# Queries, keys and gate rows stored per head for 128-row loads, y stored before values, and a new order at the start of the merge

## What is computed

```python
h = rmsnorm(x, rms_g) * (1 + scale) + shift
q, k, v, z_a, glu, z_b, gates = jnp.split(h @ w_in + b_in, PROJ_SPLITS, axis=-1)
y_a = attend(q, k, v) * jax.nn.silu(z_a)        # 8 heads of 64
y_b = conv_branch(glu, dw_w, dw_b, ln_g, ln_b) * jax.nn.silu(z_b)
g_a, g_b = jnp.split(jax.nn.sigmoid(gates), 2, axis=-1)
m = g_a * (y_a @ w_proj_a) + g_b * (y_b @ w_proj_b)
return x + gate * (m @ w_out), k, v
```

## Time and profile before

| | us |
|---|---|
| median of 3 runs | 1874.22 (1873.65 to 1875.42) |
| the profiled execution's own time | 1877.82 |
| its span, first to last instruction | 1875.6 |
| TensorE busy | 1829.8 |
| mean granted TensorE clock | 0.997 of full |

### The profile page before, as it was taken

The page is one execution under the profiler, slowest core; times in us unless marked ns, Lnnn a source line. Parts: engine busy times, 40 slices in busy tenths (PEclk is TensorE's granted clock), DMA queues, the critical chain, the costliest instruction groups (busy, mean ns, idle before and its releaser), DMA issues.

```text
span 1875.6 us, 27263 instructions
## 1 busy us (share of the span) xinstructions
PE 1829.8 (98%) x10723; PEld 1561.1 (83%) x10723; DVE 1015.1 (54%) x1710; ACT 542.0 (29%) x1061; POOL 122.8 (7%) x205
## 2 busy tenths in 40 slices
PE   6999999999999999999999999999999899999998
PEld 3788899988888888888888888888888888888886
DVE  3544512111098338816870996766768555654444
ACT  3731101021111111211110114667768222322221
POOL 0100000000000000000000004322330000000000
PEclk9999999999999999999999999999999999999999
DMA  9524423143022112211220164997887767653321
GB/s 318 169 89 158 144 68 132 49 140 115 12 78 89 65 34 82 76 40 59 72 80 20 65 153 119 211 178 163 175 182 176 229 205 244 193 191 140 141 101 56
DMA packets 211145, 235.08 MB, mean 125 GB/s; under 512 B 47707, under 2 KB 157131, under 8 KB 207819
## 3 DMA queue, kind: packets, MB, share of 16 engines
q1 hardware_dynamic: 210760, 233.24, 42.5%
q10 hardware_dynamic: 259, 0.11, 0.0%
HBM read 152.52 MB, written 80.78 MB: 124 GB/s over the span
## 4 chain that ended last, share of the span: by engine, by line
PE 90%; SPq 4%; DMA 2%; issue 1%; ACT 1%; DVE 1%; POOLq 0%; DVEq 0%; POOL 0%; ACTq 0%
PE banks L789 17%; PE banks L790 17%; PE banks L791 17%; PE banks L1742 4%; PE banks L1741 4%; PE banks L1743 4%; PE banks L1713 3%; PE banks L1715 3%; PE banks L1714 3%; PE banks L1225 3%; SPq L1093 2%; PE banks L784 2%; PE banks L785 2%; PE banks L786 2%; PE banks L1191 2%
## 5 line engine op out<-in xcount | busy, mean ns | idle before, releaser
L789 PE MATMUL banks<-h_hi,w_hi 128*128 128x512 f32 (+1 forms) x1600 | 593.3, 371 | 3.6 <-DVE h_lo L598 2.5
L790 PE MATMUL banks<-h_lo,w_hi 128*128 128x512 f32 (+1 forms) x1600 | 589.4, 368 | 0.0
L791 PE MATMUL banks<-h_hi,w_lo 128*128 128x512 f32 (+1 forms) x1600 | 589.3, 368 | 0.0
L730 DVE SCALAR_TENSOR_TENSOR conv_acc<-glu_out,taps,conv_acc 128x773 f32<-128x773 f32 x360 | 371.5, 1032 | 12.3
L789 PEld LDWEIGHTS banks<-h_hi,w_hi 128*128 128x128 f32 x1600 | 301.8, 189 | 57.6 <-issue 3.4
L791 PEld LDWEIGHTS banks<-h_hi,w_lo 128*128 128x128 f32 x1600 | 301.8, 189 | 50.7
L790 PEld LDWEIGHTS banks<-h_lo,w_hi 128*128 128x128 f32 x1600 | 302.0, 189 | 49.0
L506 ACT ACTIVATE out_stage<-banks,param_cols 128x512 f32<-128x512 f32 (+1 forms) x120 | 77.0, 647 | 439.2 <-PE banks L791 433.2
L1713 PE MATMUL banks<-y_hi,wp_hi 128*128 128x512 f32 (+1 forms) x320 | 120.0, 375 | 4.9 <-DVE m_sum L1935 2.8
L1332 ACT ACTIVATE probs<-scores,stat 128x640 f32<-128x640 f32 (+2 forms) x128 | 106.7, 834 | 60.2 <-DVE stat L1259 58.6
L1715 PE MATMUL banks<-y_hi,wp_lo 128*128 128x512 f32 (+1 forms) x320 | 118.4, 370 | 0.0
(11 more groups left out here) (161 smaller groups left out, 2397.5 us busy)
## 6 DMA issues: line engine op xcount, KB each, us to landing
proj<-out_stage SPq DMA_DIRECT2D x96, 256.0 KB, 2.0
w_raw<-in_w_in SPq DMA_DIRECT2D x44, 512.0 KB, 3.9
gates_in<-proj SPq DMA_DIRECT2D x64, 256.0 KB, 2.9
k_hi<-k_hi_rows SPq DMA_DIRECT2D x16, 640.0 KB, 13.2
k_lo<-k_lo_rows SPq DMA_DIRECT2D x16, 640.0 KB, 15.2
w_ada<-in_w_ada SPq DMA_DIRECT2D x8, 1024.0 KB, 10.8
x_out<-in_x_sample SPq DMA_DIRECT2D x16, 512.0 KB, 3.4
out_y_sample<-x_out SPq DMA_DIRECT2D x15, 512.0 KB, 2.6
```

Of the source, the lines that this page charges most:

```text
L730: op = dve.scalar_tensor_tensor(dst, src, tap, dst, ALU.mult, ALU.add)
L789: pe.matmul(out, w_hi[:, s, k], h_hi[c][:, k], start=first, stop=False)
L790: pe.matmul(out, w_hi[:, s, k], h_lo[c][:, k], start=False, stop=False)
L791: op = pe.matmul(out, w_lo[:, s, k], h_hi[c][:, k], start=False, stop=last)
```

## The change

Queries are kept in DRAM per head with the high and the low part one after the other (q_rows), keys per head and twice (k_hi and k_lo), gate rows per head with the token halves one after the other (z_rows). For this each store of 128 rows in the front becomes stores of 64 rows: queries 4 instead of 2 in a unit, keys and cached keys 8 instead of 2, gate rows 2 instead of 1 (4 in the chunk of 256). The loads of a head become one transfer of 128 rows each for q_split, k_hi, k_lo and z_halves. In a head, y of the head two earlier is stored ahead of the values. In the merge, the request for y_raw of chunk 1 moves behind the first product's store, zb_third and the last store of y behind the second, the wait for all of y to the start of chunk 1; on DVE and ACT the B branch's pairs 1 and 2 are multiplied and split later in chunk 0, and the silu of pair 0 moves ahead of the last spread of the inverse sums.

```diff
+def hi_stores(kind, col, c):
+    if kind == "z" and col < ZA0 + WA:
+        return 4 if c == 4 else 2
+    return {"q": 2, "k": 4, "ck": 4}.get(kind, 2 if kind == "v" and c == TOK // P - 1 else 1)
...
-            per_slot[slot_of[u]] += 32 if kind == "v" and c == 17 else 16
+            per_slot[slot_of[u]] += 16 * hi_stores(kind, blocks[n][1], c)
...
-            low_per_slot[lo_n % 3] += 16
+            low_per_slot[lo_n % 3] += 16 * (2 if kind == "q" else 4)
...
-    io.q_hi, io.q_lo = (nc.dram_tensor(f"q_{h}_rows", (WA, TOK), F32, kind="Internal").ap() for h in ("hi", "lo"))
-    io.k_hi, io.k_lo = (nc.dram_tensor(f"k_{h}_rows", (WA, KW), F32, kind="Internal").ap() for h in ("hi", "lo"))
+    io.q_rows = nc.dram_tensor("q_rows", (HEADS, 2, DH, TOK), F32, kind="Internal").ap()
+    io.k_hi, io.k_lo = (nc.dram_tensor(f"k_{h}_rows", (HEADS, 2, DH, KW), F32, kind="Internal").ap() for h in ("hi", "lo"))
+    io.z_rows = nc.dram_tensor("z_rows", (HEADS, 2, DH, TOK // 2), F32, kind="Internal").ap()
...
-                    sp.dma_start(hi[row:row + P, at:at + w], ohi[:, s, 0:w].bitcast(F32)).then_inc(out_d[s], 16)
-                    sp.dma_start(lo[row:row + P, at:at + w], olo[:, l, 0:w].bitcast(F32)).then_inc(low_d[l], 16)
+                    for e in range(2):
+                        part = slice(DH * e, DH * e + DH)
+                        hi, lo = ohi[part, s, 0:w].bitcast(F32), olo[part, l, 0:w].bitcast(F32)
+                        if kind == "q":
+                            sp.dma_start(io.q_rows[head + e, 0, :, at:at + w], hi).then_inc(out_d[s], 16)
+                            sp.dma_start(io.q_rows[head + e, 1, :, at:at + w], lo).then_inc(low_d[l], 16)
+                        else:
+                            for twice in range(2):
+                                sp.dma_start(io.k_hi[head + e, twice, :, at:at + w], hi).then_inc(out_d[s], 16)
+                                sp.dma_start(io.k_lo[head + e, twice, :, at:at + w], lo).then_inc(low_d[l], 16)
+                elif kind == "z" and blocks[n][1] < ZA0 + WA:
...
+                        if c < 4:
+                            sp.dma_start(io.z_rows[head + e, c % 2, :, 512 * (c // 2):512 * (c // 2) + 512],
+                                         ostg[part, s]).then_inc(out_d[s], 16)
+                        else:
+                            for half in range(2):
+                                sp.dma_start(io.z_rows[head + e, half, :, LAT // 2:TOK // 2],
+                                             ostg[part, s, P * half:P * half + P]).then_inc(out_d[s], 16)
...
-            for half in range(2):
-                part = slice(DH * half, DH * half + DH)
-                sp.dma_start(q_sp[u][part].bitcast(F32), (io.q_hi, io.q_lo)[half][rows]).then_inc(qk_in[u], 16)
-                sp.dma_start(k_hi[u][part].bitcast(F32), io.k_hi[rows]).then_inc(qk_in[u], 16)
-                sp.dma_start(k_lo[u][part].bitcast(F32), io.k_lo[rows]).then_inc(qk_in[u], 16)
+            for dst, src in ((q_sp, io.q_rows), (k_hi, io.k_hi), (k_lo, io.k_lo)):
+                sp.dma_start(dst[u][:].bitcast(F32), src[n].rearrange("h p t -> (h p) t")).then_inc(qk_in[u], 16)
...
-            for half in range(2):
-                for part in range(3):
-                    rows, tok, at = y_rows(n, half, part)
-                    src = io.proj[ZA0:ZA0 + WA][rows, tok]
-                    sp.dma_start(z_sb[DH * half:DH * half + DH, n % 2, at], src).then_inc(z_in[n % 2], 16)
+            sp.dma_start(z_sb[:, n % 2], io.z_rows[n].rearrange("h p t -> (h p) t")).then_inc(z_in[n % 2], 16)
...
-            load_v(n)
             for part in range(3):
                 store_y(sp, n - 2, part)
+            load_v(n)
...
         load_zb_pair(sp, 1)
-        io.store_last_y(sp)
-        load_zb_pair(sp, 2)
-        io.wait_y_stored(sp)
-        load_ya(sp, 1)
...
+            if og == 1:
+                load_ya(sp, 1)
+            if og == 2:
+                load_zb_pair(sp, 2)
+                io.store_last_y(sp)
             if 1 <= c < 4 and o == 0:
                 if c >= 2:
                     sp.wait_ge(mm, 16 * c)
+                else:
+                    io.wait_y_stored(sp)
                 load_ya(sp, c + 1)
...
-            if n == 1:
-                yb_high(act, 2)
+            if n == 0:
                 silu_pair(act, 2)
             if n == 5:
+                yb_high(act, 2)
+            if n == 11:
                 yb_high(act, 4)
...
-            if n in (0, 4):
-                gate_yb(dve, 2 + n // 2)
-            if n in (2, 6):
-                yb_low(dve, 2 if n == 2 else 4)
+            if n in (4, 10):
+                gate_yb(dve, 2 if n == 4 else 4)
+            if n in (6, 12):
+                yb_low(dve, 2 if n == 6 else 4)
```

The silu of pair 0 moves by a new function that the ACT program calls between copy_rest and spread of the last tile:

```diff
+    def early_silu(act, m):
+        if m == NT - 1:
+            silu_pair(act, 0)
```

More of the change, by code:

```diff
@@ L350, in front_sync @@
                 if kind in split_kinds:
-                    row = blocks[n][1] - (Q0 if kind == "q" else K0)
+                    head = (blocks[n][1] - (Q0 if kind == "q" else K0)) // DH
                     at, w = (TOK, CTX) if kind == "ck" else CHUNKS[c]
-                    hi, lo = (io.q_hi, io.q_lo) if kind == "q" else (io.k_hi, io.k_lo)
                     l = low_of[u]
-                    sp.dma_start(hi[row:row + P, at:at + w], ohi[:, s, 0:w].bitcast(F32)).then_inc(out_d[s], 16)
-                    sp.dma_start(lo[row:row + P, at:at + w], olo[:, l, 0:w].bitcast(F32)).then_inc(low_d[l], 16)
+                    for e in range(2):
[9 more added lines that the diff above has]
+                elif kind == "z" and blocks[n][1] < ZA0 + WA:
+                    head = (blocks[n][1] - ZA0) // DH
+                    for e in range(2):
+                        part = slice(DH * e, DH * e + DH)
+                        if c < 4:
[5 more added lines that the diff above has]
+                                             ostg[part, s, P * half:P * half + P]).then_inc(out_d[s], 16)
                 elif kind == "sk":
@@ L1077, in load_qk @@
                 sp.wait_ge(s_mm, TPH * (n - 1))
-            u, rows = n % 2, slice(DH * n, DH * n + DH)
-            for half in range(2):
-                part = slice(DH * half, DH * half + DH)
-                sp.dma_start(q_sp[u][part].bitcast(F32), (io.q_hi, io.q_lo)[half][rows]).then_inc(qk_in[u], 16)
-                sp.dma_start(k_hi[u][part].bitcast(F32), io.k_hi[rows]).then_inc(qk_in[u], 16)
-                sp.dma_start(k_lo[u][part].bitcast(F32), io.k_lo[rows]).then_inc(qk_in[u], 16)
+            u = n % 2
+            for dst, src in ((q_sp, io.q_rows), (k_hi, io.k_hi), (k_lo, io.k_lo)):
+                sp.dma_start(dst[u][:].bitcast(F32), src[n].rearrange("h p t -> (h p) t")).then_inc(qk_in[u], 16)
         def load_v(n):
@@ L1157, in scores @@
             if m % TPH == 0:
-                pe.wait_ge(qk_in[n % 2], 96 * (n // 2 + 1))
+                pe.wait_ge(qk_in[n % 2], 48 * (n // 2 + 1))
             if m >= 2:
@@ L1288, in gate_out @@
             if at == 0:
-                dve.wait_ge(z_in[n % 2], 96 * (n // 2 + 1))
+                dve.wait_ge(z_in[n % 2], 16 * (n // 2 + 1))
                 if n >= 2:
@@ L1360, in _ @@
                 copy_rest(m)
+                tail_stage.early_silu(act, m)
                 if m % 2:
@@ L2045, in early_act @@
             ya_high(act, 0, 1)
-        if m == NT - 1:
-            silu_pair(act, 0)
         if m == NT:
@@ L2061, in tail @@
     T.early_pe, T.early_act, T.early_dve, T.early_pool = early_pe, early_act, early_dve, early_pool
-    T.lin_done = lin_done
+    T.lin_done, T.early_silu = lin_done, early_silu
     T.load_first, T.load_wp, T.load_ya = load_ln_first, load_wp, load_ya
```

## The result

| | before | after |
|---|---|---|
| median of 13 runs each, us | 1875.22 (1873.55 to 1877.53) | 1878.95 (1875.48 to 1880.11) |
| the profiled execution's own time | 1877.82 | 1878.72 |
| its span | 1875.6 | 1876.6 |

The ratio after to before is 1.0017, 95% interval 1.0009 to 1.0025: the change made the kernel slower by 0.17%, or 3.2 us, little but clear of zero. The forecast was 5.2 us faster, so the sign was wrong, though the time lies just inside the range (its upper end was 1879). A small difference hides three large ones, and four marks in the trace split them: the first store of values (up to there TensorE has waited for nothing that the change touches), the first scores (the start of attention), the first matmul of the merge, and the first of the output projection.

A forecast was written before the change was run, and what follows sets the result against it. TensorE, busy 98% of the span, was taken as the bound. From the profiled 1877.8 us, + 6.0 (stores) - 6.2 (head loads) - 5.0 (merge) = 1872.6, put at 1869.0 for the median; range 1862.5 to 1879.

The forecast's parts named there:

- Part 1, loads of a head: Attention: wider, fewer loads and earlier y stores remove the waits for v_ctx, k_lo and y_halves, saving 6.2 us.
- y is stored ahead of the values: Attention: stores land some 30 us before DVE reuses y_halves; 3.67 us of issues ahead of values, less than 5 gained.
- ACT and DVE will take some back: Attention: next in line to hold TensorE, they reduce the saving from 5.8 to 7.2 us of waits to 6.2.
- the rival built on it: Attention: ACT's exponents or DVE's minima hold TensorE instead, only 2 of 6.2 us remain, 1873.2 us; chance 0.13.
- Part 2, start of the merge: Merge start: reordering saves 2.8 for m_sum, 1.7 for the clock and 0.9 for silu, less 0.4: 5.0 us.
- I charge 0.4: Merge: y_raw of chunk 1, requested later near 1467, is split about when TensorE reaches chunk 1, costing 0.4 us.
- the 1.7 for the clock: Merge: 1.7 us come back if the low clock after the m_sum wait, 0.66 from 1471 to 1476, does not occur.
- Part 3, the stores: Front, key blocks 2 to 4: 64-row stores at 0.64 us make SyncE's queue fall behind, costing 6.0 us.
- Block 1 has seventeen light units behind it: Front, block 1: its added stores cause no wait, as seventeen light units follow; 0 us.
- 1.1 us to spare: Front, block 3: the copy is ready at 419.1 against TensorE's 420.2, so no wait.
- The first rival: Front: the new wait, near 4 us in one piece, lowers the clock, adding 1.7 us, 1870.7 us; chance 0.15.
- It is close but the issues decide: Front: the 112 stores and other loads need 66 us of DMA time within 73.5 us of issues, so issues set the time.

The follow-up runs named there:

- e3: The changed kernel with the values loaded ahead of the stores of y, as before: 1879.37 us, ratio to before 1.0011.
- e1: The changed kernel with all hunks on stores, layouts and loads taken back; y ahead of values and new merge order stay: 1871.27 us, ratio to before 0.9969.
- e2: The changed kernel with the old order of SyncE, VectorE and ScalarE in the merge's first chunk: 1881.3 us, ratio to before 1.0029.
- e6: The changed kernel with y_raw of chunk 1 requested right behind zb_second, ahead of the merge's loop: 1877.27 us, ratio to before 1.0004.
- f2: The changed kernel with both copies of 64 key rows written by one transfer, four issues a key unit instead of eight: 1864.85 us, ratio to before 0.9943.
- g3: The changed kernel with low key copies in one transfer and high ones in two, six issues a key unit: 1866.59 us, ratio to before 0.9955.
- f3: The changed kernel with the four low stores of a key unit issued on ACT's queue: 1872.52 us, ratio to before 0.998.
- e4: The changed kernel with stores as before, one copy, and 128-row loads reading it in place with a first dimension of two: 2350.52 us, ratio to before 1.2526.

## Why the prediction was wrong, point by point

**Part 1, loads of a head: right in sign, too small.** Forecast 6.2, measured 8.3. All named waits went, and sixteen v_win issues now take 12.3 us (at 1211.18) in place of 20.9. The reasons were half right: the rates of the earlier trace rows carried it (8.3 us with the wide loads alone by e3, 6.2 on top of the new order by e1), while "y is stored ahead of the values" was worth 2.1 alone and nothing beside the wide loads. "ACT and DVE will take some back" didn't happen, and neither did the rival built on it.

**Part 2, start of the merge: the gain came, and two thirds of it went again.** Forecast 5.0, measured 1.9 (1.7 by e2). Compare the start of the same matmul in both traces, counted from the first of the merge. At 1473 us it is 5.2 us sooner than before: 0.8 by the first silu, 2.8 by m_sum, 1.6 by the clock, where the forecast had 0.9, 2.8 and 1.7. Then 1.8 are lost behind the new wait for m_sum and 1.4 behind those for the low part of y_raw.
- One step that failed is the price of the late request for y_raw, "I charge 0.4": it cost the 1.8 of m_sum. The sum looked at y_raw's own landing and not at what was queued behind that megabyte, the fifth pair of gates. e6 shows it: with y_raw asked for earlier, that wait goes and the merge is 2.5 us shorter. The request itself came at 1472.07, where the sum had it near 1467, or 1469.7 with the 2.7 us by which DVE's first product starts later here. It took the gated products as back to back, but the second waited 2.57 us for its gates, at 1469.23.
- The other is the 1.7 for the clock. The fall was no property of the old order (e2), and its end is hardly a gain: the old order without it waits 1.9 us for the low part of y_raw, the new one 2.0, and before, slowed by the clock, 0.9. The next wait takes what the clock gives back, all but 0.3.

**Part 3, the stores: the step that turned the sign.** Forecast +6.0, measured +11.5 (11.7, 11.9 and 13.5 in e6, e2 and e3). The sum had the last wait right and put three others at nothing: the units right behind block 1, block 3, and the clock. Counted from the first value store, the same matmul starts later than in before by 2.3 us ahead of block 2, 3.4 at 429 us (block 3), 5.7 at 445, 10.1 at 455 and 11.5 at 459 us. So 2.3 + 1.1 + 6.7 + 1.4 = 11.5, and each term has its place:
- "Block 1 has seventeen light units behind it" failed: +2.3, forecast 0. Light units behind don't help the units next to it. ACT waits 7.21 us for the store of a slot of block 1, until 321.41, and DVE's value copy at 331.61 waits 3.45 us for a store of values that stood behind the key stores. TensorE waits 1.0 and 0.7 us, and block 2 starts 2.3 us late.
- Block 3: +1.1, forecast 0. The sum found 1.1 us to spare (0.6, had it counted the issue of state_k); with the late start it was 0.2 and 0.4 us of waiting, and each wait costs more than its idle time, as the first matmul behind it takes 0.50 us in place of 0.39.
- Block 4: +6.7, forecast 6.0. The wait at the transposed keys was right. ACT wrote the copy at 454.35 instead of 450.7: 1.8 us for the later start of the stores (376.66 for 374.84), and 1.8 for two issues that took 1.59 and 1.45 us in place of 0.64, which no row had shown. TensorE waited 2.05 and 4.16 us there.
- The clock: +1.4. The first rival, given 0.15 and priced at 1.7, happened: 0.72 in 455 to 460 us.
- Price and pace were right: 0.60 and a gap of 0.04, with one pause of 0.35 between 376.66 and 469.38.

**The other limit.** "It is close but the issues decide" holds for the changed kernel: the same bytes in fewer issues cost nothing (f2, g3). The room behind was small, 0.60 us from landing to landing in f3 against 0.64 from issue to issue.

**The base.** By the two profiled executions the change is +0.9 (+1.3 by stages, -0.4 by the start); the medians say +3.7, the ratio of runs +3.2. Before's profiled execution stood 2.6 above its median, and after's at it. The forecast had allowed for that (3.6), so this is no part of the miss. But some 2 us of the ratio lie in no stage of this pair. Starts differ by up to 3.1 us, and the fronts of four kernels with the same stores by 2.0; what the rest is stays open.

## What to carry to other kernels

Cost a store not only by its engine time but by the queue in front of the narrowest place, unit by unit: if what a unit issues takes longer than the unit, the debt grows until a slot holds the engine (here 8 issues of 64 rows cost 11.5 us, and 6 cost none, since their debt of 3.6 us stayed within the slots). When loads want their data twice, let the store write both copies in one transfer with the rows outermost (f2), and don't put a dimension of two outermost (e4). When a large request is moved, ask what small one stands behind it; and compare short stages between marks in the trace, since the start of a kernel can vary by more than the change does.

## What was not expected of the hardware

- A 128-row load whose source has an outermost dimension of two ran at 53 GB/s with a DMA share of 0.13 (e4).
- Issues of 64-row stores at 0.64 us are interrupted by one of 1.4 to 1.6 us, five times in the four key blocks of the changed kernel (303.37, 321.52, 397.54, 424.06, 457.02 us). What it is stays open.
- Two queues at once issued eight 64-row stores in 3.3 us, 0.41 each against 0.64 from one, but they landed one per 0.60 us (f3).
- The granted clock fell to its 1.2 GHz level for a while after idle times of TensorE of 2.8 us (before), 4.2 (after), 3.6 (f3), 2.2 in block 4 of e3 and 1.9 in attention (e1, to a mean of 0.69 in 5 us). It did not after 2.6 us (e2), 2.4 in the merge of e3, 2.3 (e1) or 2.05 (after, at 445 us): the length of the wait alone doesn't decide it.
